# Four weight blocks a conditioning step, and a router with stationary weights in two column halves

## The chip, the cores and the metric

The kernel runs on one NeuronCore of a Trainium2 chip. The metric is the device time of one execution in microseconds; lower is better. Everything is float32. In the trace a float32 product on TensorE (PE) leaves two matmul records, a transpose one.

## The reference

Two layers of a hybrid backbone over 256 latent and 256 context tokens, 1024 wide. The two parts that the change touches are the conditioning and the router:

```python
s_lat = jax.nn.silu(c)
s_ctx = jax.nn.silu(c_ctx)
...
    mod = (s_lat @ ada_w[l] + ada_b[l])[:, None, :]
    mod_c = s_ctx @ ada_w[l] + ada_b[l]
    shift_a, scale_a, gate_a, shift_f, scale_f, gate_f = jnp.split(mod, 6, axis=-1)
...
    scores = jax.nn.sigmoid((t @ router).astype(jnp.float32))
    _, idx = lax.top_k(scores + bias.astype(jnp.float32), TOP_K)
```

`ada_w[l]` is 1024 x 6144, 24 MB a layer, and multiplies two vectors only: the conditioning of the latents and that of the context. `router` is 1024 x 64, for 512 tokens in layer 0 and 256 in layer 1. Each layer normalises, modulates and projects, runs three token mixers (retention, attention, gated MLP) that gated merges bring together, projects out, and ends with 64 small experts of which each token takes 6.

## The kernel before, in words

Activations lie feature by token: `xT` and `hT` hold 8 blocks of 128 features by 512 tokens. `layer_steps` writes out one order of steps for each layer; the five engines run it, each its own part. A step's products go into a bank of PSUM (a job); `jobs` numbers them, job n uses bank n % 8, and PE waits in `open_bank` until job n-8 has been emptied by ACT or DVE. `bank_full` counts finished jobs.

Weights come through `ring`, nine slots of 1 MB (`NS`), in order of first use, block p into slot p % 9. The SP queue loads block p only when the last step that used block p-9 has filled its bank (`await_free`), in order. Experts use the same ring after that.

Conditioning is done in steps `adaw` and `adat` (`step_adaw`, L748, and `step_adat`, L757, on PE). Before the change a layer has twelve of each. `adaw` takes two blocks of 256 columns. `silu_c` (two columns of conditioning, padded to 32) is stationary, the block is moving; the eight k-tiles go round the four column groups of 32, so that each group holds a partial sum of two k-tiles. ACT copies the bank to `ada_row` (128 x 512). `adat` multiplies each 128 columns of `ada_row` (stationary) by `sel`, which adds the four partial sums and turns the row into 128 partitions x 2. DVE adds `ada_b` into `mod` (L1534). The first norm of layer 0 needs the first 16 blocks of 128 of `mod`. In layer 0 four steps stand at the start among the turns of x (L670) and the mean squares (L700), eight in attention (`spread` and `weave` mix them with the branch-2 merges), and the twelve of layer 1 stand in the retention and branch-1 merges of layer 0.

```python
    if l + 1 < DEPTH:
        bulk = weave(ada_steps(l + 1, list(range(12))), bulk)
    out += spread([("ret", n) for n in range(len(ret_units(l)) + 2)], bulk)
```

The router (`step_rt`, L950) takes 128 tokens of `hT` as stationary and 64 columns of `router` as moving, 8 k-tiles a token tile. ACT makes `score` of the bank with tanh. Behind it PE turns `hT` for the expert rows (`h2`, L670) and does the shared expert (`sg`, `su`, `sd`), while DVE picks the experts.

Of the kernel before, what the change touches and what calls it, by code (L numbers as in the profile page):

```python
# [27 lines left out]
P = 128  # L28
# [34 lines left out]
CONST_COLS = {"ident": P, "iota1": P, "diff": 384, "tri": P, "tok": 8, "cos": 2 * ROPE, "sin": 2 * ROPE, "sel": 2}  # L63
# [17 lines left out]
def shape_constants():  # L81

    out = np.zeros((P, N_CONST), np.float32)

    def put(name, a):
        out[:, CONST_AT[name]:CONST_AT[name] + CONST_COLS[name]] = a

    p = np.arange(P)
    put("ident", np.eye(P))
    put("iota1", np.broadcast_to(np.arange(P) + 1, (P, P)))  # L90
    put("diff", np.arange(384)[None, :] - P - p[:, None])
    put("tri", (p[:, None] < p[None, :]))
    put("sel", (p[:, None] % 32 == np.arange(2)[None, :]))
# [52 lines left out]
def layer_steps(l):  # L146
# [22 lines left out]
    if l == 0:  # L169
        bulk = weave(ada_steps(0, list(range(4, 12))), bulk)  # L170
# [9 lines left out]
    out += [("out", m) for m in range(8)] + [("ms2",), ("norm", 2), ("rt",)] + [("h2", t) for t in mt]  # L180
# [9 lines left out]
def step_jobs(l, kind, *a):  # L190
# [42 lines left out]
    return [((kind, l) + a, "act" if kind in ("q", "k", "g", "ws", "u", "gv", "rt", "sg", "ms1", "ms2") else "dve")]  # L233


def step_pieces(l, kind, *a):

    if kind == "adaw":
        return [(a[0], "ada", 2 * a[1] + i) for i in range(2)]
# [16 lines left out]
    return {"ws": [(l, "ws")], "rt": [(l, "router")], "sg": [(l, "sg")], "su": [(l, "su")], "sd": [(l, "sd")]}.get(kind, [])  # L256


def backbone(nc, dram, out):
# [29 lines left out]
    with ExitStack() as ctx:  # L289
# [14 lines left out]
        ada_row = sb("ada_row", [P, 512])  # L304
# [103 lines left out]
        y_parts = [region(0, TOPK * D), region(15872, TOPK * D)]  # L408
        fin = region(0, 2, D)
# [256 lines left out]
        def _(pe):  # L666
# [52 lines left out]
            for l in range(DEPTH):  # L719
# [19 lines left out]
                def step_adaw(la, q):  # L739
# [3 lines left out]
                    for i in range(2):  # L743
                        p = piece_at[(la, "ada", 2 * q + i)]
                        await_loaded(pe, p)
                        for k in range(KT):
                            g = 32 * (k % 4)
                            last = mm(b[g:g + 32, 256 * i:256 * i + 256], silu_c[:, k, :], piece_view(p, KT, 256)[:, k, :],  # L748
                                      start=(k < 4), stop=(k >= 4))
                    last.then_inc(bank_full, 1)  # L750

                def step_adat(la, q):
# [3 lines left out]
                    for m in range(4):  # L756
                        last = mm(b[:, 2 * m:2 * m + 2], ada_row[:, P * m:P * m + P], const_cols("sel"), start=True, stop=True)  # L757
# [233 lines left out]
                def step_list(e):  # L991
# [3 lines left out]
                    for i in range(len(mt)):  # L995
# [7 lines left out]
                         "rt": step_rt, "h2": step_h2, "sg": shared("sg"), "su": shared("su"), "sd": step_sd, "pos": step_pos,  # L1003
# [149 lines left out]
        def _(act):  # L1153
# [54 lines left out]
            for l in range(DEPTH):  # L1208
# [15 lines left out]
                def step_adaw(la, q):  # L1224
                    if q or la:
                        await_full(act, ("adat", la, q - 1) if q else ("adat", la - 1, 11))
                    copy_out(("adaw", la, q), ada_row[:, :])
# [132 lines left out]

                def step_rt():
# [13 lines left out]
                def step_sg(m):  # L1375
# [5 lines left out]
                            "k": step_k, "g": step_g, "ret": step_ret, "out": step_out, "ms2": step_ms2, "norm": step_norm, "rt": step_rt, "h2": step_h2,  # L1381
# [53 lines left out]
        def _(dve):  # L1435
# [76 lines left out]
            for l in range(DEPTH):  # L1512
# [15 lines left out]
                def step_adat(la, q):  # L1528

                    if la == 0 and q == 0:  # L1530
                        await_emptied(dve, ("vec", 1))
                    b = await_full(dve, ("adat", la, q))
                    at = VEC_AT["ada_b"] + 4 * q
                    link(v.tensor_tensor(mod[:, la, 4 * q:4 * q + 4, :], b[:, 0:8].rearrange("p (m s) -> p m s", s=2),  # L1534
                                         vec[:, la, at:at + 4].unsqueeze(2).to_broadcast([P, 4, 2]), ALU.add))
                    dve.nop().then_inc(emptied["dve"], 1)
                    for g, name, first in ((gain1, "n1", 8), (gain2, "n2", 32)):
                        if 4 * q + 4 == first + KT:
# [3 lines left out]
                    if 4 * q + 4 == 24:  # L1542
# [501 lines left out]
```

## Time and profile before

| | us |
|---|---|
| median of 3 runs | 2792.06 (2790.34 to 2795.26) |
| span of the profiled execution | 2791.2 |
| PE busy (matmul) | 2423.6 (87%) |
| DVE busy | 764.5 (27%) |
| ACT busy | 482.0 (17%) |
| mean granted TensorE clock | 0.914 |

For the profiled execution only its span is listed, and no time of its own beside it. By stage, in us from the span's start: start and first norm 0 to 75, latents and first projections to 237, attention with branch-2 merges to 399, retention projections to 509, retention with branch-1 merges to 652, branch-0 merges and out projection to 811, router and shared expert to 877, experts to 1700, layer 1 up to its router to 2081, its experts from 2116 to the end.

A row of the timeline gives start, duration, engine, line, operation, output and inputs, the count that it merges, and in brackets the idle time of the engine before it with what ended it. Granted clock 1.00 is 2.4 GHz, 0.50 is 1.2 GHz.

### The profile page before, as it was taken

How to read it: one execution, taken by the hardware profiler on the slowest of the kernel's cores; microseconds unless marked ns; L12 is line 12 of the kernel's file. 1: busy time of each engine (PE TensorE's matmuls, PEld its weight loads, DVE VectorE, ACT ScalarE, POOL GpSimd, SP SyncE). 2: the span in 40 equal slices, each digit the busy share in tenths (PEclk: the TensorE clock that was granted, in tenths of full speed). 3: DMA queues.
4: the chain of work that ended last, by engine and by line, in shares of the span. 5: the costliest groups of instructions: out<-in, count | busy, mean ns of one | idle time of the engine just before them, and what ended most of it. 6: DMA issues, size and time to landing. Idle time of an engine off the chain costs nothing.

```text
span 2791.2 us, 39130 instructions
## 1 busy us (share of the span) xinstructions
PE 2423.6 (87%) x13062; PEld 1605.6 (58%) x13063; DVE 764.5 (27%) x2357; ACT 482.0 (17%) x1015; POOL 272.8 (10%) x320
## 2 busy tenths in 40 slices
PE   4997999999988988888888869899988778787876
PEld 3665556554455555556665567677876445444545
DVE  2324320231133323222223223431323222222221
ACT  3331111120020111111111113320221111111110
POOL 1000000000001111111111120000001111111111
PEclk9998999999989888999998889999999888888888
DMA  8132452464224888788878850432446888888884
GB/s 277 46 109 64 130 166 68 147 202 154 83 89 148 329 317 342 286 319 305 311 267 312 303 218 31 136 114 68 131 152 252 328 333 333 338 331 333 333 332 177
DMA packets 219213, 608.19 MB, mean 218 GB/s; under 512 B 22027, under 2 KB 152277, under 8 KB 169973
## 3 DMA queue, kind: packets, MB, share of 16 engines
q1 hardware_dynamic: 191584, 541.62, 53.5%
q0 software_dynamic: 26128, 61.07, 6.1%
q10 hardware_dynamic: 1412, 4.28, 0.4%
q8 instruction: 60, 0.98, 0.1%
q14 instruction: 29, 0.23, 0.0%
HBM read 596.94 MB, written 35.00 MB: 226 GB/s over the span
## 4 chain that ended last, share of the span: by engine, by line
PE 69%; DMA 15%; issue 6%; DVE 4%; POOLq 3%; ACT 2%; DVEq 1%; POOL 0%; ACTq 0%; SPq 0%
PE bank L677 25%; DMA area<-h_rows,idx 14%; PE bank L1044 11%; PE bank L685 6%; PE bank L670 6%; PE bank L1076 5%; PE bank L1051 2%; POOLq L548 2%; PE bank L1052 2%; PE bank L714 2%; PE bank L748 2%; DVE area L1876 1%; PE bank L824 1%; PE bank L802 1%; PE bank L839 1%
## 5 line engine op out<-in xcount | busy, mean ns | idle before, releaser
L1044 PE MATMUL bank<-ring,area 128*64 128x256 f32 x1840 | 530.1, 453 | 23.4 <-issue 19.9
L1045 PE MATMUL bank<-ring,area 128*64 128x256 f32 x1840 | 530.2, 453 | 0.0
L677 PE MATMUL bank<-hT,ring 128*128 128x512 f32 (+1 forms) x1408 | 481.1, 498 | 0.0
L670 PE MATMUL bank<-const,area 128*128 128x128 f32 (+3 forms) x1668 | 256.9, 301 | 227.8 <-DMA area<-h_rows,idx 183.9
L1044 PEld LDWEIGHTS bank<-ring,area 128*64 128x64 f32 x1840 | 291.8, 165 | 210.8 <-issue 125.3
L677 PEld LDWEIGHTS bank<-hT,ring 128*128 128x128 f32 x1408 | 265.6, 191 | 192.0 <-issue 176.3
L670 PEld LDWEIGHTS bank<-const,area 128*128 128x128 f32 (+3 forms) x1668 | 218.2, 189 | 266.2 <-issue 222.7
L1045 PEld LDWEIGHTS bank<-ring,area 128*64 128x64 f32 x1840 | 291.7, 165 | 0.0
L1076 PE MATMUL bank<-ring,area 128*64 128x512 f32 (+1 forms) x1024 | 267.2, 596 | 3.3 <-issue 2.5
L1956 POOL DMA_INDIRECT area<-h_rows,idx x130 | 123.6, 951 | 1425.6 <-DVEq L1826 1306.4
L677 PE MATMUL bank<-area,ring 128*128 128x512 f32 (+1 forms) x704 | 237.8, 486 | 2.8 <-issue 2.8
L1863 DVE SCALAR_TENSOR_TENSOR area<-area,wrow,bank 64x256 f32<-64x256 f32 (+1 forms) x128 | 61.7, 482 | 635.6 <-ACT area L1397 504.2
L1962 POOL DMA_INDIRECT expert_rows<-area,idx x128 | 118.1, 923 | 1034.5 <-issue 1034.5
L677 PEld LDWEIGHTS bank<-area,ring 128*128 128x128 f32 x704 | 133.4, 190 | 96.3 <-issue 87.3
L685 PE MATMUL bank<-ring,hT 128*128 128x256 f32 (+1 forms) x800 | 166.9, 370 | 6.2 <-ACT hT L1204 6.2
L685 PEld LDWEIGHTS bank<-ring,hT 128*128 128x128 f32 x800 | 147.4, 192 | 28.5 <-ACT hT L1204 6.3
L1397 ACT ACTIVATE area<-bank 128x256 f32<-128x256 f32 (+1 forms) x128 | 48.8, 381 | 645.5 <-PE bank L1045 505.4
L1173 ACT ACTIVATE area<-bank 128x512 f32<-128x512 f32 (+1 forms) x122 | 60.9, 505 | 517.5 <-PE bank L677 417.7
L1076 PEld LDWEIGHTS bank<-ring,area 128*64 128x64 f32 (+1 forms) x1024 | 84.6, 143 | 111.6 <-issue 96.9
L1854 DVE COPY area<-bank 128x512 f32<-128x512 f32 (+1 forms) x128 | 71.5, 558 | 229.7 <-PE bank L670 220.6
L1019 PEld LDWEIGHTS bank<-area 128*128 128x128 f32 (+1 forms) x756 | 86.5, 173 | 81.4 <-issue 81.2
L1393 ACT ACTIVATE area<-bank 128x512 f32<-128x512 f32 (+1 forms) x128 | 62.8, 491 | 375.9 <-PE bank L670 365.1
(192 smaller groups left out, 2039.4 us busy)
## 6 DMA issues: line engine op xcount, KB each, us to landing
ring<-in_moe_w_gate SPq DMA_DIRECT2D x128, 1024.0 KB, 7.0
ring<-in_moe_w_up SPq DMA_DIRECT2D x128, 1024.0 KB
ring<-in_moe_w_down SPq DMA_DIRECT2D x128, 1024.0 KB
ring<-in_w_in SPq DMA_DIRECT2D x52, 1024.0 KB, 7.9
ring<-in_ada_w SPq DMA_DIRECT2D x48, 1024.0 KB, 11.5
area<-expert_rows POOLq DMA_DIRECT2D x36, 512.0 KB, 7.6
ring<-in_w_out SPq DMA_DIRECT2D x8, 1024.0 KB, 9.0
ring<-in_w_br_gmlp SPq DMA_DIRECT2D x8, 512.0 KB, 8.4
```

Source lines behind the costliest of these rows:

```text
L670: return nc.tensor.transpose(dst, src, ident[0:n, 0:n])
L677: last = mm(b[:, 0:n], lhs[:, k, :], rhs[:, k, c:c + n], start=(k == 0), stop=(k == K - 1))
L685: last = mm(b[:, 0:n], lhs[:, k, P * tt:P * tt + P], rhs[:, k, :], start=(k == 0), stop=(k == K - 1))
L1019: last = mm(bank[7][0:cap, 256:259], pick[:, j, P * i:P * i + cap], entry(i, e), start=(i == 0), stop=(i == nm - 1))
L1044: mm(bank[4 + j][0:P // 2, 0:FF], x, wg[:, k, :], start=(k == 0), stop=(k == KT - 1))
L1045: last = mm(bank[4 + j][P // 2:P, 0:FF], x, wu[:, k, :], start=(k == 0), stop=(k == KT - 1))
L1076: last = mm(bank[2 + hf][o * hf:o * hf + m, :], hidT[:, j, cap * k:cap * k + m], wd[:, k, 512 * hf:512 * hf + 512], start=(k == 0), stop=( ...
L1393: af(x_rowsT[:, j, 0:4 * cap], bank[0][:, 0:4 * cap], ACT.Copy).then_inc(turned_act, 1)
L1854: v.tensor_copy(x_rowsT[:, j, 4 * cap:8 * cap], bank[1][:, 0:4 * cap]).then_inc(turned_dve, 1)
L1863: v.scalar_tensor_tensor(out=hid[0:m, j, :], in0=act_g[0:m, j, :], scalar=wrow[0:m, j:j + 1], in1=up, op0=ALU.mult, op1=ALU.mult).then_inc ...
L1956: pool.indirect_dma_start(out=x_rows[0:m, j, :], out_offset=None, in_=h2_dram[0:tokens(l), :], in_offset=bass.IndirectOffsetOnAxis(ap=idx[ ...
L1962: pool.indirect_dma_start(out=y_dram[0:TOPK * tokens(l), :], out_offset=bass.IndirectOffsetOnAxis(ap=idx[0:m, j, 2:3], axis=0), in_=y_rows ...
```

## The change

There are six conditioning steps a layer instead of twelve (`ADA_STEPS`). A step takes four blocks, one for each column group: all eight k-tiles of block i accumulate in partitions 32i to 32i+31, 256 columns wide. PE waits for all four blocks before the first product. `ada_row` is 128 x 256, and two products with a `sel` of eight columns turn 1024 values; DVE adds the bias in two operations. At the start x0 and x1 are turned ahead of the first step, both mean squares stand together, and the second step behind them. Elsewhere `spread` and `weave` mix six steps where they mixed twelve.

The router becomes two steps. In `lt` the router's 64 columns are stationary and the tokens move; even k-tiles go to column half 0, odd ones to half 1. ACT copies the bank to `logits`. In `rt` each 128 tokens of `logits` are stationary against `fold`, which adds the two halves and turns them back to token by expert.

```diff
-        ada = ada_steps(0, list(range(4)))
-        out += [("vec",)] + ada[:2] + [("x", 0), ("x", 1)] + ada[2:4] + [("x", 2), ("x", 3), ("ms1", 0)] + ada[4:6]
-        out += [("ms1", 1)] + ada[6:] + [("norm", 0), ("norm", 1)]
+        ada = ada_steps(0, list(range(2)))
+        out += [("vec",), ("x", 0), ("x", 1)] + ada[:2] + [("x", 2), ("x", 3), ("ms1", 0), ("ms1", 1)] + ada[2:]
+        out += [("norm", 0), ("norm", 1)]
...
-        bulk = weave(ada_steps(0, list(range(4, 12))), bulk)
+        bulk = weave(ada_steps(0, list(range(2, ADA_STEPS))), bulk)
...
-        bulk = weave(ada_steps(l + 1, list(range(12))), bulk)
+        bulk = weave(ada_steps(l + 1, list(range(ADA_STEPS))), bulk)
...
-        return [(a[0], "ada", 2 * a[1] + i) for i in range(2)]
+        return [(a[0], "ada", 4 * a[1] + i) for i in range(4)]
...
-                    for i in range(2):
-                        p = piece_at[(la, "ada", 2 * q + i)]
+                    quarters = [piece_at[(la, "ada", 4 * q + i)] for i in range(4)]
+                    for p in quarters:
                         await_loaded(pe, p)
-                        for k in range(KT):
-                            g = 32 * (k % 4)
-                            last = mm(b[g:g + 32, 256 * i:256 * i + 256], silu_c[:, k, :], piece_view(p, KT, 256)[:, k, :],
-                                      start=(k < 4), stop=(k >= 4))
+                    for k in range(KT):
+                        for i, p in enumerate(quarters):
+                            last = mm(b[32 * i:32 * i + 32, 0:256], silu_c[:, k, :], piece_view(p, KT, 256)[:, k, :],
+                                      start=(k == 0), stop=(k == KT - 1))
...
-                    for m in range(4):
-                        last = mm(b[:, 2 * m:2 * m + 2], ada_row[:, P * m:P * m + P], const_cols("sel"), start=True, stop=True)
+                    for m in range(2):
+                        last = mm(b[:, 8 * m:8 * m + 8], ada_row[:, P * m:P * m + P], const_cols("sel"), start=True, stop=True)
...
-                def step_rt():
+                def step_lt():
+
                     pe.wait_ge(h_ready, norm_at(("ms2", l)) + 1)
                     p = piece_at[(l, "router")]
                     await_loaded(pe, p)
+                    b = open_bank(pe, ("lt", l))
+                    for k in range(KT):
+                        g = N_EXP * (k % 2)
+                        last = mm(b[g:g + N_EXP, 0:nt], piece_view(p, KT, N_EXP)[:, k, :], hT[:, k, t0:T], start=(k < 2), stop=(k >= KT - 2))
+                    last.then_inc(bank_full, 1)
+
+                def step_rt():
+
+                    await_emptied(pe, ("lt", l))
                     b = open_bank(pe, ("rt", l))
-                    for i, t in enumerate(mt):
-                        for k in range(KT):
-                            last = mm(b[:, N_EXP * i:N_EXP * i + N_EXP], hT[:, k, P * t:P * t + P], piece_view(p, KT, N_EXP)[:, k, :],
-                                      start=(k == 0), stop=(k == KT - 1))
+                    for i in range(len(mt)):
+                        last = mm(b[:, N_EXP * i:N_EXP * i + N_EXP], logits[:, P * i:P * i + P], const_cols("fold"), start=True, stop=True)
                     last.then_inc(bank_full, 1)
...
+                def step_lt():
+                    copy_out(("lt", l), logits[:, 0:nt], lambda b: b[:, 0:nt])
```

How the rows of PE move, in three places. A row names line, operation, output and inputs, size, and how many follow each other.

PE at the start, before: the block products of `adaw` (L748) and turning products of `adat` (L757) among the turns of x (L670) and mean squares (L700).

```order
L748 MATMUL bank<-ring,silu_c 32x256 x16
L757 MATMUL bank<-const,ada_row 128x2 x4
L670 MATMUL bank<-const,area 128x128 x16
L748 MATMUL bank<-ring,silu_c 32x256 x16
L757 MATMUL bank<-const,ada_row 128x2 x4
L670 MATMUL bank<-const,area 128x128 x16
L700 MATMUL bank<-area,ones 128x256 x8
L748 MATMUL bank<-ring,silu_c 32x256 x16
L757 MATMUL bank<-const,ada_row 128x2 x4
L700 MATMUL bank<-area,ones 128x256 x8
L748 MATMUL bank<-ring,silu_c 32x256 x16
L757 MATMUL bank<-const,ada_row 128x2 x4
```

The same place now (L751, L760, L673 and L703 are the same four lines).

```order
L673 MATMUL bank<-const,area 128x128 x16
L751 MATMUL bank<-ring,silu_c 32x256 x32
L760 MATMUL bank<-const,ada_row 128x8 x2
L673 MATMUL bank<-const,area 128x128 x16
L703 MATMUL bank<-area,ones 128x256 x16
L751 MATMUL bank<-ring,silu_c 32x256 x32
L760 MATMUL bank<-const,ada_row 128x8 x2
```

The first turns of x have moved ahead of the first step, and no step stands between the two mean squares.

PE in the branch-1 merges of layer 0, before: a merge is L677 x8 (gate) and x4 (branch); L909, L921 and L670 are a retention step.

```order
L757 MATMUL bank<-const,ada_row 128x2 x4
L748 MATMUL bank<-ring,silu_c 32x256 x16
L757 MATMUL bank<-const,ada_row 128x2 x4
L677 MATMUL bank<-hT,ring 128x512 x8
L677 MATMUL bank<-area,ring 128x512 x4
L909 MATMUL bank<-area 128x256 x4
L921 MATMUL bank<-area 128x128 x4
L670 MATMUL bank<-const,area 128x128 x2
L748 MATMUL bank<-ring,silu_c 32x256 x16
L757 MATMUL bank<-const,ada_row 128x2 x4
```

And now, from merge 1 to the third step and merge 2.

```order
L680 MATMUL bank<-hT,ring 128x512 x8
L680 MATMUL bank<-area,ring 128x512 x4
L760 MATMUL bank<-const,ada_row 128x8 x2
L912 MATMUL bank<-area 128x256 x4
L924 MATMUL bank<-area 128x128 x4
L673 MATMUL bank<-const,area 128x128 x2
L751 MATMUL bank<-ring,silu_c 32x256 x32
L680 MATMUL bank<-hT,ring 128x512 x8
```

A step directly followed by its own turning products occurs twice in this stage now, four times before.

PE at the router of layer 0, before: L950 is the router, L670 the turns of h2, the last row the shared expert.

```order
L677 MATMUL bank<-area,ring 128x512 x8
L700 MATMUL bank<-area,ones 128x512 x2
L950 MATMUL bank<-ring,hT 128x64 x32
L670 MATMUL bank<-const,hT 128x128 x32
L677 MATMUL bank<-hT,ring 128x512 x16
```

The same place now, with L954 for `lt` and L962 for the folding.

```order
L680 MATMUL bank<-area,ring 128x512 x8
L703 MATMUL bank<-area,ones 128x512 x2
L954 MATMUL bank<-hT,ring 64x512 x8
L962 MATMUL bank<-const,area 128x64 x4
L673 MATMUL bank<-const,hT 128x128 x32
L680 MATMUL bank<-hT,ring 128x512 x16
```

Thirty-two products became eight and four, with a copy by ACT between them. On ACT the table load for tanh stood directly behind the last operation on `hT`; it now stands behind this copy.

## Rows read from the trace of the kernel before

**Rows 1.** The page, chain that ended last: share of the span by engine.

```profile
PE 69%; DMA 15%; issue 6%; DVE 4%; POOLq 3%; ACT 2%; DVEq 1%; POOL 0%; ACTq 0%; SPq 0%
```

**Rows 2.** Timeline of PE in the branch-1 merges of layer 0.

```profile
587.06 1.02 PE L757 MATMUL bank<-const,ada_row 128*128 128x2 f32 x8 [0.87 <-ACT ada_row L1173]
588.01 1.93 PE L748 MATMUL bank<-ring,silu_c 128*32 128x256 f32 x32
589.88 1.13 PE L909 MATMUL bank<-area 128*128 128x256 f32 x4
...
603.15 0.95 PE L757 MATMUL bank<-const,ada_row 128*128 128x2 f32 x8
604.03 1.93 PE L748 MATMUL bank<-ring,silu_c 128*32 128x256 f32 x32
```

**Rows 3.** Timeline of PE at the routers of layers 0 and 1.

```profile
811.36 13.91 PE L950 MATMUL bank<-ring,hT 128*128 128x64 f32 x64 [11.64 <-ACT hT L1204]
825.07 5.07 PE L670 MATMUL bank<-const,hT 128*128 128x128 f32 x32
...
2087.75 3.44 PE L670 MATMUL bank<-const,hT 128*128 128x128 f32 x16
```

**Rows 4.** Timeline of the start, PE, ACT and DVE.

```profile
27.13 1.93 PE L748 MATMUL bank<-ring,silu_c 128*32 128x256 f32 x16 [12.01 <-DMA ring<-in_ada_w]
...
39.24 1.95 PE L670 MATMUL bank<-const,area 128*128 128x128 f32 x16
...
41.28 0.71 ACT L1192 ACTIVATE area<-xT 128x256 f32<-128x256 f32 x2
...
49.22 0.71 ACT L1192 ACTIVATE area<-xT 128x256 f32<-128x256 f32 x2
...
55.20 1.93 PE L748 MATMUL bank<-ring,silu_c 128*32 128x256 f32 x32
...
59.06 0.17 DVE L1534 TENSOR_TENSOR mod<-bank,vec 128x8 f32<-128x8 f32 x1 [8.36 <-PE bank L757]
...
65.25 10.00 PE L685 MATMUL bank<-ring,hT 128*128 128x256 f32 x35 [6.23 <-ACT hT L1204]
```

**Rows 5.** The experts' products in column halves, and their weight loads.

```profile
2121.76 0.38 PE L1044 MATMUL bank<-ring,area 128*64 128x256 f32 x1
2121.76 0.38 PE L1045 MATMUL bank<-ring,area 128*64 128x256 f32 x1
...
1505.60 1.89 PE L1076 MATMUL bank<-ring,area 128*64 128x512 f32 x8
...
L1076 PEld LDWEIGHTS bank<-ring,area x1024: 132/137/338, 891.6 to 2746.9; 128*64 128x64 f32 x152, 128*128 128x128 f32 x19
```

**Rows 6.** Fourth block and x: issue, and time to landing (last number).

```profile
10.41 11.39 SPq L644 DMA_DIRECT2D ring<-in_ada_w  x1
...
DMA to landing us min/median/max: 22.7/22.7/22.7
...
8.79 0.72 POOL L1941 DMA_DIRECT2D area<-in_x  x1
...
area<-in_x POOLq DMA_DIRECT2D x1, 1024.0 KB, 11.2
```

**Rows 7.** Timeline of PE in attention, 256 keys, two steps back to back.

```profile
277.45 0.41 PE L670 MATMUL bank<-const,area 128*128 128x128 f32 x2 [0.40 <-ACT area L1304]
```

**Rows 8.** DMA issues, median us to landing: 380 to 520 us, then 500 to 660 us.

```profile
ring<-in_ada_w SPq DMA_DIRECT2D x10, 1024.0 KB, 5.5
...
ring<-in_ada_w SPq DMA_DIRECT2D x18, 1024.0 KB, 11.2
```

**Rows 9.** Windows: stretch, length, busy by engine, granted clock, DMA share, GB/s.

```profile
65.00:70.00 5.00, 4.75 (x11) 3.85 (x12) 4.55 (x9) 3.35 (x9) 0.00 (x0) 0.50 0.01 2
70.00:75.00 5.00, 5.00 (x25) 4.37 (x25) 0.54 (x2) 0.15 (x1) 0.00 (x0) 0.98 0.00 0
...
815.00:820.00 5.00, 5.00 (x26) 5.00 (x25) 0.00 (x0) 0.00 (x0) 0.00 (x0) 0.50 0.00 0
```

More of the change, by code:

```diff
@@ L62 @@
 ROW_BC = {"qn": QK, "kn": NOPE, "kr": ROPE, "lng": GW, "lnb": GW, "bs": GW, "bias": N_EXP, "dec": 8}
-CONST_COLS = {"ident": P, "iota1": P, "diff": 384, "tri": P, "tok": 8, "cos": 2 * ROPE, "sin": 2 * ROPE, "sel": 2}
+CONST_COLS = {"ident": P, "iota1": P, "diff": 384, "tri": P, "tok": 8, "cos": 2 * ROPE, "sin": 2 * ROPE, "sel": 8, "fold": N_EXP}
+ADA_STEPS = 6
 def offsets(sizes):
@@ L92, in shape_constants @@
     put("tri", (p[:, None] < p[None, :]))
-    put("sel", (p[:, None] % 32 == np.arange(2)[None, :]))
+    put("sel", (p[:, None] == 32 * (np.arange(8)[None, :] // 2) + np.arange(8)[None, :] % 2))
+    put("fold", (p[:, None] % N_EXP == np.arange(N_EXP)[None, :]))
     tok = np.arange(TT)[None, :] * P + p[:, None] - BIG
@@ L176, in layer_steps @@
     if l + 1 < DEPTH:
-        bulk = weave(ada_steps(l + 1, list(range(12))), bulk)
+        bulk = weave(ada_steps(l + 1, list(range(ADA_STEPS))), bulk)
     out += spread([("ret", n) for n in range(len(ret_units(l)) + 2)], bulk)
     out += [("merge", m, 0) for m in range(8)]
-    out += [("out", m) for m in range(8)] + [("ms2",), ("norm", 2), ("rt",)] + [("h2", t) for t in mt]
+    out += [("out", m) for m in range(8)] + [("ms2",), ("norm", 2), ("lt",), ("rt",)] + [("h2", t) for t in mt]
     out += [("sg", m) for m in range(2)] + [("pos",), ("cnt",)] + [("su", m) for m in range(2)]
@@ L232, in step_jobs @@
         return []
-    return [((kind, l) + a, "act" if kind in ("q", "k", "g", "ws", "u", "gv", "rt", "sg", "ms1", "ms2") else "dve")]
+    return [((kind, l) + a, "act" if kind in ("q", "k", "g", "ws", "u", "gv", "lt", "rt", "sg", "ms1", "ms2") else "dve")]
 def step_pieces(l, kind, *a):
     if kind == "adaw":
-        return [(a[0], "ada", 2 * a[1] + i) for i in range(2)]
+        return [(a[0], "ada", 4 * a[1] + i) for i in range(4)]
     if kind == "c":
@@ L255, in step_pieces @@
         return [(l, "wo", a[0] // 2)]
-    return {"ws": [(l, "ws")], "rt": [(l, "router")], "sg": [(l, "sg")], "su": [(l, "su")], "sd": [(l, "sd")]}.get(kind, [])
+    return {"ws": [(l, "ws")], "lt": [(l, "router")], "sg": [(l, "sg")], "su": [(l, "su")], "sd": [(l, "sd")]}.get(kind, [])
 def backbone(nc, dram, out):
@@ L303, in backbone @@
         silu_c = sb("silu_c", [P, KT, 32])
-        ada_row = sb("ada_row", [P, 512])
+        ada_row = sb("ada_row", [P, 256])
         mod = sb("mod", [P, DEPTH, 48, 2])
@@ L1225, in step_adaw @@
                     if q or la:
-                        await_full(act, ("adat", la, q - 1) if q else ("adat", la - 1, 11))
-                    copy_out(("adaw", la, q), ada_row[:, :])
+                        await_full(act, ("adat", la, q - 1) if q else ("adat", la - 1, ADA_STEPS - 1))
+                    copy_out(("adaw", la, q), ada_row[:, :], lambda b: b[:, 0:256])
                 def step_ms1(s):
@@ L1532, in step_adat @@
                     b = await_full(dve, ("adat", la, q))
-                    at = VEC_AT["ada_b"] + 4 * q
-                    link(v.tensor_tensor(mod[:, la, 4 * q:4 * q + 4, :], b[:, 0:8].rearrange("p (m s) -> p m s", s=2),
-                                         vec[:, la, at:at + 4].unsqueeze(2).to_broadcast([P, 4, 2]), ALU.add))
+                    at = VEC_AT["ada_b"] + 8 * q
+                    for m in range(2):
+                        last = v.tensor_tensor(mod[:, la, 8 * q + m:8 * q + 8:2, :], b[:, 8 * m:8 * m + 8].rearrange("p (i s) -> p i s", s=2),
+                                               vec[:, la, at + m:at + 8:2].unsqueeze(2).to_broadcast([P, 4, 2]), ALU.add)
+                    link(last)
                     dve.nop().then_inc(emptied["dve"], 1)
                     for g, name, first in ((gain1, "n1", 8), (gain2, "n2", 32)):
-                        if 4 * q + 4 == first + KT:
+                        if 8 * q + 8 == first + KT:
                             n_g = vec[:, la, VEC_AT[name]:VEC_AT[name] + KT].unsqueeze(2).to_broadcast([P, KT, 2])
```

7 lines of the change are left out of this document (4 added, 3 removed).

## The prediction

> **What bounds the kernel now.** I read the chain of waits first: 69% of the span lies on the matmul queue and 15% on DMA [rows 1]. Most of that is attention, projections and experts, which the change leaves alone. So the question is local: where do the conditioning steps and the router stand on the matmul queue, and does PE wait there or work? A change of 0.2% (5.6 us) is about what a measurement of this kernel can tell from none.
>
> Then the rows of the conditioning code. The turning products, `ada_row` against `sel`, are 96 in the run, four in each of 24 steps. Four of them hold PE from 603.15 to 604.03, so 0.22 us each [rows 2], although only 2 columns move. They cost that because each loads a full 128-column stationary. The reader should see the same in the router: 64 records of 64 moving columns fill 13.9 us [rows 3].
>
> Third, the start, which is a chain. PE idles until the second weight block has landed at 27.13, takes that half step at half speed (8 products in 1.93 us, where 16 take 1.93 at 55.20), turns x, squares, and ends with `mod` at 59.06; the first projection begins at 65.25 [rows 4]. Fourth, the branch-1 merges of layer 0 (509 to 652 us): PE has work throughout, and its only waits near conditioning are of 0.87 us, where a turning product follows its own step at once [rows 2].
>
> **The change, part by part.** The blocks multiplied stay 384 products per run, four column groups in rotation before and after. A step of 16 takes 1.87 us in the stream (588.01 to 589.88 [rows 2]). Four products at once need 0.43, two passes of 256 columns at 0.21 each, as the experts' 512 columns in halves (8 records in 1.89 [rows 5]) give them, so 1.71 of it is streaming and 0.15 is paid once per step. A new step is then 3.42 + 0.15 = 3.57 us. Ten of the steps that go lie outside the start, so 1.5 us of the gain below are this overhead.
>
> *Start: +2.0 us.* Steps 0 and 1 now need four blocks each. The fourth block was issued at 10.41 and landed 22.7 later, at 33.1 [rows 6]; before, PE could begin at 27.13. x was issued at 8.8 and landed 11.2 later, at 20.0 [rows 6], so its first 16 turns move into the idle time ahead and are off the path. From 33.1: 32 products at half speed 7.2 (four times the 1.93 less its tails); copy and hand-over 0.65; two turning products 0.6; this gives 41.6. Turning x2 and x3 to the first square took 2.04 (39.24 to 41.28), so squares begin at 43.7, against 41.28. The two norms now follow each other with no step between. The second took 6.0 us, from 49.22 to the step at 55.20; the first 7.9, with the copy of a step in it [rows 4]; between the two I take 6.4. So the last step begins at 56.1, takes 3.57, then copy and two products 1.3: `mod` at 61.0 against 59.06. If the clock rises inside the first step it is +0.8; if DMA lands later, +4.
>
> *Attention of layer 0: -4.2.* Eight steps become four: 24 turning products fewer, 24 x 0.22 = -5.2; four step overheads, -0.6. Against that, bulk now follows each second attention step. With 256 keys a step is too short to cover ACT's softmax, and where two stand back to back PE waited 0.40 [rows 7]. Such pairs go from one to five: +1.6. With 512 keys I charge nothing: ACT and DVE finish under the longer step.
>
> *Branch-1 merges: -6.0.* Twelve steps become six: 36 products fewer, -7.8; six overheads, -0.9. A turning product stands directly behind its step twice, not four times, and the copy is half as wide, for which I take 0.65 where PE idled 0.87: 4 x 0.87 less 2 x 0.65 = -2.2. The new cost is the ring. It has nine slots and block p loads when block p-9 is done. The fourth block of the third step takes the slot of the gate weights of merges 0 and 1, free only after merge 1. Between that and the step lie two turning products and one retention step: 0.44, four products of 256 columns at 0.43, four of 128 at 0.22, two turns at 0.11, 3.3 us and 3.4 with hand-overs. A block issued to an idle queue lands in 5.5 us [rows 8]. So PE waits 2.0. The fourth block of the last step waits for merge 5 in the same way, with two turning products, eight of 128 columns and two turns between, 2.5 us: it waits 2.9. Together +4.9. Every other step has a whole merge, 12 products of 512 columns or 10.3 us, between the freeing of its last block and its start. The upper bound is the median of this stage, 11.2 us [rows 8], taken with queued loads: 7.8 + 8.7 = 16.5. The lower is 0. I take 5.5, since the queue has been served by then. Behind a waiting step stand only merges, whose weights land 3 us behind the late block and before it ends.
>
> *Router of layer 0: -7.1.* 32 products took 811.36 to 825.07, 13.7 us, at a granted clock of 0.50 (the 1.2 GHz level) to the end [rows 3, 9]. Now 8 products of 512 columns go in two column halves. Four such products take 1.8 us in the experts at full clock [rows 5], so 3.4, at half 6.8. After its idle time before 65.25 the clock stood at 0.50 up to 70 us, under dense work, and at 0.98 from 70 to 75 [rows 9]; with the same here the eight take 5.9. Then ACT copies (0.9 with the hand-over, PE idle), and four folding products take 0.9. The turns of h2 start at 819.0 instead of 825.07. They then run at full clock, 3.9 instead of 4.9. The table load for tanh, formerly hidden, falls behind the copy: 1.3 beside 0.9 of folding, so tanh ends at 819.6, not late for anything on PE. If the clock stays at half all through, only -2.
>
> In the Trainium skill, TensorE: Matmul & The Clock Gate, Part 3, weight loads overlap running matmuls only if their row groups differ; all these share the 128 rows. By that rule the 16 loads of 137 ns [rows 5] would add 2.2 us in each layer. The trace disagrees: four products of this form take 1.89 with their eight loads, of which 1.71 is streaming.
>
> *Router of layer 1: -2.5.* Half as many products, 16, took half as long, 6.9, up to 2087.75. Now 3.6 + 0.65 + 0.9 = 5.1, so -1.8; and the 16 turns behind (3.44 [rows 3]) may meet the higher clock earlier, at most -1.5 more. I take half of that. ACT's and DVE's own savings cost PE nothing and give nothing: both are mostly idle.
>
> Sum: 2.0 - 4.2 - 6.0 - 7.1 - 2.5 = **-17.8 us**. Later stages should shift as a whole, because expert weights cannot run ahead by more than nine blocks. The profiled span is 2791.2, 0.9 below the median of the runs, 2792.06, so I subtract from the median: **2774.3 us**.
>
> **Rivals.** *The ring starves PE* for the 16.5 us above: -17.8 - 4.9 + 16.5 = -6.2, and if each wait drops the clock for 5 us, another +5: 2785.9 to 2790.9. For: four blocks now come free at once. Against: no row of before has PE waiting for a block after the start.
>
> *The router keeps half the clock*: gain 2 in layer 0 and 1.8 in layer 1, so -12.0: 2780. For: it stayed at 0.50 through the old router. Against: dense columns raised it at 70.
>
> *Weight loads of the router are not hidden*: if each of its 16 loads of 137 ns stood between two products in both layers, +4.4, so 2778.7. Against: four products with eight loads take 1.89 [rows 5], which leaves no room for 1.1 of loads. This is the skill's rule above.
>
> *The column groups no longer run together*, the case on the slower side. Each group now streams from another slot of the ring. If only two overlapped, 32 products would take 16 x 0.43 = 6.8 us, +3.3 on each of 12 steps, +39: 2813. It decides for slower once a step takes over 3.57 + 17.8/12 = 5.1. Against: the experts' gate and up products read two slots and start together at 2121.76 [rows 5].
>
> **How the numbers follow.** Forecast 0.72, half clock in the router 0.12, starved ring 0.10, unhidden loads 0.02, groups apart 0.04. The likeliest gives 2774.3. Its own bounds are the start (-1.2 to +2), ring (-4.9 to +4), clock in the routers (-2 to +6), some 2768 to 2783; with part of the starved case, and a little for what I have not seen, 2766 to 2786. Faster: the forecast, the clock and loads cases and a little of the starved one, 0.88; same 0.08; slower 0.04.
>
> **What would show it.** A step of 32 products near 3.6 us and a pair of turning products near 0.44. `mod` complete near 61. Waits for ring blocks of 2 to 3 us ahead of the third and last step of the branch-1 merges, and nowhere else after the start. The router's eight products at some 6 us with h2's turns starting 7.6 us after them. The forecast is wrong if a step takes over 5 us, if PE waits for blocks in attention, or if the time between router and experts does not shrink.

## The result, and the profile after

The changed kernel takes 2770.47 us (median of 6 runs, 2758.21 to 2781.14) where the kernel before took 2793.66 beside it (6 runs, 2785.84 to 2799.33). The ratio is 0.9923, 95% interval 0.99 to 0.9946. The profiled execution took 2771.84, with a span of 2769.5 at a mean granted clock of 0.921. The forecast was 2774.3.

The page first: busy time by engine, and the chain that ended last by engine. It answers to [rows 1].

```profile
PE 2380.8 (86%) x12866; PEld 1568.4 (57%) x12867; DVE 763.1 (28%) x2357; ACT 472.3 (17%) x1005; POOL 271.9 (10%) x320
...
PE 68%; DMA 16%; issue 6%; DVE 4%; POOLq 3%; ACT 2%; DVEq 1%; POOL 0%; ACTq 0%; SPq 0%
```

PE is busy 43 us less than before (2423.6), and the span is 22 us shorter. The two differ, so the page alone doesn't say where the time went; stage marks on PE's timeline do. In us, from the same instruction to the same instruction of both profiles:

| stretch | before | after | difference | forecast |
|---|---|---|---|---|
| to the first projection | 65.25 | 65.48 | +0.2 | +2.0 |
| first projection to first attention score | 140.37 | 139.76 | -0.6 | 0 |
| first attention score to first retention product | 303.33 | 304.28 | +0.95 | -4.2 |
| first retention product to router of layer 0 | 302.41 | 298.01 | -4.4 | -6.0 |
| router of layer 0 | 18.61 | 11.68 | -6.9 | -7.1 |
| shared expert and lists of layer 0 | 47.34 | 47.34 | 0 | 0 |
| experts of layer 0 to router of layer 1 | 1203.6 | 1196.4 | -7.2 | 0 |
| router of layer 1 | 10.17 | 6.22 | -3.95 | -2.5 |
| from there to the end | 700.17 | 700.37 | +0.2 | 0 |

The row of 1200 us is code that the change leaves alone. PE is busy for 1066.6 us of it before and for 1049.4 after, at a mean granted clock of 0.92 and 0.93. In nine more profiles below, one of them with the old router and one with the old conditioning, it takes 1191.9 to 1201.0. So the 1196.4 of the change is ordinary, and the 1203.6 of before is the longest of eleven. Of the kernel before there is one profile only; whether its 7 us are chance is not shown. The runs of one kernel differ by more: the six of the change lie 23 us apart.

PE's timeline at the start, answering to [rows 4]:

```profile
20.14 3.68 PE L673 MATMUL bank<-const,area 128*128 128x128 f32 x16 [11.56 <-DMA area<-in_x]
33.36 6.20 PE L751 MATMUL bank<-ring,silu_c 128*32 128x256 f32 x64 [9.54 <-DMA ring<-in_ada_w]
40.05 0.61 PE L760 MATMUL bank<-const,ada_row 128*128 128x8 f32 x4 [0.50 <-ACT ada_row L1184]
...
54.27 3.66 PE L751 MATMUL bank<-ring,silu_c 128*32 128x256 f32 x64
58.59 0.58 PE L760 MATMUL bank<-const,ada_row 128*128 128x8 f32 x4 [0.66 <-ACT ada_row L1184]
```

The fourth block arrived at 33.36 (forecast 33.1) and x's turns lie ahead of it in what was idle time. A step of 32 products takes 3.66, within 0.1 of the 3.57 worked out. The copy of the half-wide row leaves PE idle 0.66, for which 0.65 had stood.

PE's timeline in the branch-1 merges, answering to [rows 2]: six steps, two of which wait for the ring.

```profile
550.89 3.66 PE L751 MATMUL bank<-ring,silu_c 128*32 128x256 f32 x64 [2.25 <-DMA ring<-in_ada_w]
...
581.43 3.66 PE L751 MATMUL bank<-ring,silu_c 128*32 128x256 f32 x64
585.75 0.58 PE L760 MATMUL bank<-const,ada_row 128*128 128x8 f32 x4 [0.66 <-ACT ada_row L1184]
...
621.93 5.35 PE L751 MATMUL bank<-ring,silu_c 128*32 128x256 f32 x64 [2.96 <-DMA ring<-in_ada_w]
627.21 7.13 PE L680 MATMUL bank<-hT,ring 128*128 128x512 f32 x16
...
637.83 0.51 PE L760 MATMUL bank<-const,ada_row 128*128 128x8 f32 x4
638.20 1.96 PE L680 MATMUL bank<-hT,ring 128*128 128x512 f32 x4
```

The third and the last step wait 2.25 and 2.96 for their blocks, as forecast (2.0 and 2.9). But the same 64 records take 5.35 behind the second wait. The window there, with the columns of [rows 9], shows why: the granted clock is 0.54 with PE fully busy.

```profile
622.00:625.00 3.00, 3.00 (x32) 1.86 (x36) 0.28 (x1) 0.00 (x0) 0.00 (x0) 0.54 1.10 350
```

PE's timeline at the two routers, answering to [rows 3]:

```profile
807.53 6.54 PE L954 MATMUL bank<-hT,ring 128*64 128x512 f32 x16 [11.63 <-ACT hT L1215]
814.77 1.10 PE L962 MATMUL bank<-const,area 128*128 128x64 f32 x8 [0.70 <-ACT area L1184]
815.71 3.66 PE L673 MATMUL bank<-const,hT 128*128 128x128 f32 x32
...
2062.91 3.49 PE L954 MATMUL bank<-hT,ring 128*64 128x256 f32 x16 [6.67 <-ACT hT L1215]
2066.88 0.66 PE L962 MATMUL bank<-const,area 128*128 128x64 f32 x4 [0.49 <-ACT area L1184]
2067.37 1.92 PE L673 MATMUL bank<-const,hT 128*128 128x128 f32 x16
```

13.9 us of products with 64 moving columns have become 6.54, 0.70 of idle time and 1.10. The turns of `hT` behind them take 3.66 where they took 5.07, because the clock had risen inside the eight products: it stood at 0.50 up to 812.5 and at 1.00 from 813.5.

### The profile page after: what moved, and what is told of

The parts are those of the page before. It is cut to its first block, busy times and chain, and to the rows that moved or that the text cites. A ratio compares the mean times of both kernels' runs of the same rounds, so it can differ in the third digit from the quotient of the medians.

```text
span 2769.5 us, 38705 instructions
## 1 busy us (share of the span) xinstructions
PE 2380.8 (86%) x12866; PEld 1568.4 (57%) x12867; DVE 763.1 (28%) x2357; ACT 472.3 (17%) x1005; POOL 271.9 (10%) x320
## 4 chain that ended last, share of the span: by engine, by line
PE 68%; DMA 16%; issue 6%; DVE 4%; POOLq 3%; ACT 2%; DVEq 1%; POOL 0%; ACTq 0%; SPq 0%
PE bank L680 25%; DMA area<-h_rows,idx 14%; PE bank L1055 11%; PE bank L688 6%; PE bank L673 6%; PE bank L1087 5%; POOLq L551 2%; PE bank L1062 2%; PE bank L751 2%; PE bank L717 2%; PE bank L1063 2%; DVE area L1892 1%; DMA ring<-in_ada_w 1%; PE bank L827 1%; PE bank L805 1%
## 5 line engine op out<-in xcount | busy, mean ns | idle before, releaser
L1055 PE MATMUL bank<-ring,area 128*64 128x256 f32 x1840 | 514.0, 442 | 22.2 <-issue 22.1
L1056 PE MATMUL bank<-ring,area 128*64 128x256 f32 x1840 | 514.2, 442 | 0.0
L673 PE MATMUL bank<-const,area 128*128 128x128 f32 (+3 forms) x1668 | 261.2, 304 | 254.8 <-DMA area<-h_rows,idx 197.4
L1055 PEld LDWEIGHTS bank<-ring,area 128*64 128x64 f32 x1840 | 285.0, 161 | 200.8 <-issue 111.5
L673 PEld LDWEIGHTS bank<-const,area 128*128 128x128 f32 (+3 forms) x1668 | 220.1, 189 | 295.6 <-issue 236.3
L1056 PEld LDWEIGHTS bank<-ring,area 128*64 128x64 f32 x1840 | 284.9, 161 | 0.0
```

The source lines that it names most:

```text
L673: return nc.tensor.transpose(dst, src, ident[0:n, 0:n])
L1055: mm(bank[4 + j][0:P // 2, 0:FF], x, wg[:, k, :], start=(k == 0), stop=(k == KT - 1))
L1056: last = mm(bank[4 + j][P // 2:P, 0:FF], x, wu[:, k, :], start=(k == 0), stop=(k == KT - 1))
```

## Experiments

**Repeating the change.** To know how far profiles of one kernel differ, the changed kernel ran again.

> The changed kernel, once more. Theory 1: the steps outside the experts take the same time in every execution but for the granted clock, and the 7.3 us by which layer 0's experts were shorter than before came from the clock by chance; so the start of the first projection, the start of retention, the end of the branch-1 merges and the router repeat within 3 us (65.5, 509.5, 648.7, 11.7 long), while the 823 us of experts differ by several us either way. Theory 2: the shorter experts' stage is an effect of the change; then it repeats, 7 us shorter than before's. Time by both 2758 to 2781.

Measured: 2770.32 (2768.17 to 2779.83, 6 runs), ratio 0.9932 [0.9908, 0.9956]. Attention stretch 304.19 and ring waits 2.07 and 2.83 repeat. The routers differ by the clock alone: layer 0 takes 10.12 instead of 11.68, because the clock rose 3 us earlier, and layer 1 takes 8.49 instead of 6.22, because it stayed at 0.50 until the turns were done. The expert stretch takes 1199.65, 3.3 longer than in the first profile.

**One part alone.** First the conditioning without the router:

```diff
-... ("norm", 2), ("lt",), ("rt",)] + [("h2", t) for t in mt]
+... ("norm", 2), ("rt",)] + [("h2", t) for t in mt]
...
-                    for i in range(len(mt)):
-                        last = mm(b[:, N_EXP * i:N_EXP * i + N_EXP], logits[:, P * i:P * i + P], const_cols("fold"), start=True, stop=True)
+                    for i, t in enumerate(mt):
+                        for k in range(KT):
+                            last = mm(b[:, N_EXP * i:N_EXP * i + N_EXP], hT[:, k, P * t:P * t + P], piece_view(p, KT, N_EXP)[:, k, :],
```

> Conditioning as changed, router as before. Theory 1: the router and h2's turns take 18.6 us in layer 0 and 10.2 in layer 1 again, 10.9 more than with the change, so about 12 us of the 23 remain: 2781, ratio 0.995 to 0.997. Rival (the conditioning is worth nothing, since attention began retention no earlier than before and the ring gave back the rest): 2789 to 2794, ratio 1.00.

Measured: 2784.02 (2775.19 to 2788.35, 12 runs), ratio 0.997 [0.9955, 0.9984], so about 8 us. Then the router without the conditioning (`adaw`, `adat`, `ada_steps` and `sel` as before, `lt` and `fold` added):

> Router as changed, conditioning as before. Theory 1: 11.7 us from the router to the end of h2's turns in layer 0 where 18.6 stood, 6.2 in layer 1 where 10.2 stood, nothing else moves: -10.9, so 2783, ratio 0.996. Rival (the router carries all of the gain): -22, ratio 0.992.

Measured: 2778.94 (2763.35 to 2787.26, 12 runs), ratio 0.9955 [0.9935, 0.9975], so about 12 us. Taken from the ratios the parts are 8.4 and 12.6 us, 21.0 in sum, and both together 21.5 and 19.0 in the two sets of runs: within the intervals they add. Forecast were 8.2 and 9.6. The intervals (4.5 to 12.6 us, and 7.0 to 18.1) are too wide to judge a term by; the stages do that. The retention stretch shrinks by 4.75 (302.41 to 297.66) with the new conditioning alone and by nothing with the new router alone (302.41), the router of layer 0 goes to 11.14 with the new router alone and stays at 18.13 without it.

**Freeing the gate slot earlier.** Are the waits of 2.25 and 2.96 due to the ring slot of the gate weights? A merge has two jobs, the gate product first. The edit lets that slot go after the first.

```diff
-                last_use[piece] = len(jobs) - 1
+                last_use[piece] = len(jobs) - 1 - (piece[1] == "gate")
```

> The changed kernel, with the slot of a merge's gate weights given back when the gate product is full and not when the branch product is, 3.4 us earlier. Theory 1: the waits for ring blocks of 2.25 and 2.96 us ahead of the third and the last step of the branch-1 merges go to 0, and with them the fall of the clock that followed the second (5.35 us for a step that takes 3.66): 5 to 7 us less than the change from 509.5 to 648.7, 132 to 134 where it took 139.2; time 2763 to 2766. Rival (the waits come from the DMA rate, not from when the slot is free): the two waits stay above 1.5 us each and the time stays at 2770.

Measured: 2761.47 (2759.01 to 2775.76, 6 runs), ratio 0.991 [0.9883, 0.9937]. PE's timeline at the same two steps:

```profile
540.86 3.66 PE L751 MATMUL bank<-ring,silu_c 128*32 128x256 f32 x64
...
608.88 3.66 PE L751 MATMUL bank<-ring,silu_c 128*32 128x256 f32 x64
```

Both waits are gone and so is the 5.35. From the first retention product to the router it takes 290.98 instead of 298.01: 7.0 us, of which 5.2 are the waits and 1.7 the slow step. The same kernel once more:

> The kernel with the gate slot freed early, again, beside the one with the spread attention. Theory 1: no wait for ring blocks after the start, branch-1 merges in 121.3 us to the last turning product where the change takes 128.3; time 2760 to 2766. Rival (its 9 us under the change were the clock of one set of runs): 2770.

Measured: 2765.18 (2758.0 to 2776.08, 6 runs), ratio 0.9922 [0.9899, 0.9945]; the stretch 290.98 again, in a profile of 2756.1. So the stage gains 7 us, while the medians of the runs, 2761 and 2765 against 2770, are 5 to 9 lower and their intervals overlap with the change's: for the whole kernel this edit is shown by the profiles, not by the ratios.

**One group after the other.** Do the four column groups run together because neighbours in the instruction stream are in different groups?

```diff
-                    for k in range(KT):
-                        for i, p in enumerate(quarters):
+                    for i, p in enumerate(quarters):
+                        for k in range(KT):
```

> The changed kernel, with the 32 products of a conditioning step in another order: all eight k-tiles of block 0 in column group 0, then those of block 1 in group 1, and so on, so that neighbours share a group. Theory 1 (the four groups run together because neighbours lie in different groups): 32 x 0.43 = 13.7 us a step instead of 3.6, +10 us on each of 12 steps less the 5 us of ring waits, which the longer steps cover: 2880 to 2895. Rival (PE overlaps the groups whatever the order, or did not overlap them before): a step stays at 3.6 us and the time at 2770.

Measured: 2866.94 (one run). PE's timeline:

```profile
582.39 11.50 PE L751 MATMUL bank<-ring,silu_c 128*32 128x256 f32 x64
612.70 11.47 PE L751 MATMUL bank<-ring,silu_c 128*32 128x256 f32 x64 [2.16 <-DMA ring<-in_ada_w]
```

The clock is 1.00 in the first of these rows. The groups are not even fully apart: the recorded expectation for that was 13.7, and why it is 2.2 less stays open. 32 products in this order take 11.5 us where they take 3.66 in rotation: 7.8 more, and twelve steps of that are 94 of the 96.5 us by which the kernel is longer. The rival in which the groups fall apart thus has its price, and by which edit it would come. The ring waits stay (2.16 here, 2.96 at the last step, at 707.21), though every step is 8 us longer: they depend only on what lies between the merge that frees the slot and the step that needs the block.

**The router in one half.** Is the router's gain the new orientation (`router` stationary, 512 tokens moving) or the two column halves? The copy and the folding, not shown here, use 64 partitions accordingly.

```diff
-                        g = N_EXP * (k % 2)
-                        last = mm(b[g:g + N_EXP, 0:nt], ..., start=(k < 2), stop=(k >= KT - 2))
+                        last = mm(b[0:N_EXP, 0:nt], ..., start=(k == 0), stop=(k == KT - 1))
```

> The changed kernel, with the router's eight products all in column half 0 (64 partitions), then folded from 64 partitions. Theory 1 (the split halves the products' time): they take 9 to 10 us in layer 0 where 6.5 stood and 6 in layer 1 where 3.5 stood, +5 in all. Rival (the gain of the router comes from the exchange of the operands alone): 6.5 and 3.5 us again.

Measured: 2776.52 (one run). PE's timeline at both routers:

```profile
809.35 9.86 PE L953 MATMUL bank<-hT,ring 128*64 128x512 f32 x16 [11.63 <-ACT hT L1214]
...
2069.19 6.27 PE L953 MATMUL bank<-hT,ring 128*64 128x256 f32 x16 [6.67 <-ACT hT L1214]
```

9.86 and 6.27 stand against 6.54 and 3.49, so in these profiles the halves are worth 3.3 and 2.8 us. But the clock differs between the forms. Windows, first of the kernel before, then of this one:

```profile
811.36:825.07 13.71, 13.71 (x65) 13.71 (x65) 0.00 (x0) 1.25 (x1) 0.00 (x0) 0.50 0.00 0
```

```profile
809.35:815.00 5.65, 5.65 (x7) 1.67 (x8) 0.00 (x0) 0.00 (x0) 0.00 (x0) 0.50 0.00 0
815.50:819.20 3.70, 3.70 (x9) 0.96 (x7) 0.00 (x0) 0.00 (x0) 0.00 (x0) 1.00 0.00 0
```

Count each microsecond at full clock twice, which puts everything at half clock, and the old form takes 13.9 us in layer 0 and 7.1 in layer 1, this one 14.1 and 7.2, and the two halves 7.3 and 3.8. At one clock the orientation thus brings nothing and the halves bring it all, although the weight loads (the second busy time of a row) fill the whole window of the old form and only 1.67 of 5.65 us here. The 4.1 us between 13.91 and 9.86 are the clock's: with the tokens moving it rose 2.6 to 5.8 us behind the router's first product of layer 0, in ten profiles; with the old router, in two, 15.5 and 16.6 us behind it. That is an association. It doesn't hold in layer 1, where in five of the nine profiles with two halves the clock stayed at 0.50 about as long as with the old router.

**Spreading the attention.** The stretch that had not gained is attention. In the change `spread` puts 16 bulk steps behind 30 attention steps, so behind every second one; before it was 24. Now the first 12 of the 30, which have 256 keys, get one each, and the 18 behind them the other four. Nothing is added or left out; only the order differs. This edit alone, on the change:

```diff
-    out += att[:4] + [("sv", t) for t in mt] + spread(att[4:], bulk)
+    n = 12 if l == 0 else 0
+    out += att[:4] + [("sv", t) for t in mt] + spread(att[4:4 + n], bulk[:n]) + spread(att[4 + n:], bulk[n:])
```

It ran first together with the freed gate slot:

> The kernel with the gate slot freed early, and in layer 0's attention a merge, a block step or a turning pair behind each of the twelve next attention steps with 256 keys, the last four such pieces over the 18 steps with 512. Theory 1 (two short attention steps back to back let PE wait for the softmax, and those waits are 0.4 to 0.6 us each): the five waits on ACT go, 2 to 3 us less before retention begins, and the clock falls in attention are fewer; 2758 to 2761. Rival (the waits move elsewhere or the clock falls are not tied to them): attention takes as long as in the kernel before this one, 2761 to 2764.

Measured: 2747.8 (2744.94 to 2751.1, 5 runs), ratio 0.9844 [0.9825, 0.9864]: 10 us below what the better theory had for it (2758 to 2761). A repeat:

> Spread attention and the gate slot freed early, again. Theory 1: the stretch of attention repeats at 290 us and the branch-1 merges at 121.3; time 2745 to 2752, 5 to 7 below the kernel with the spread alone. Rival (its 2748 was the clock of one set): 2755 to 2762.

Measured: 2750.46 (2744.63 to 2754.15, 5 runs), ratio 0.9854 [0.9834, 0.9874]. And the new order without the freed slot:

> The changed kernel with the spread attention alone, the gate slot given back as in the change. Theory 1 (what attention earned was lost to its own order: waits and the clock falls around them): from the first attention score to the start of retention 290 to 292 us where the change took 304.3, with at most 20 us at half clock where it had 37.5; the two ring waits in the branch-1 merges stay at 2 and 3 us; time 2753 to 2758. Rival (the clock in attention is chance, as it is among the experts): 298 to 304 us for that stretch and 2763 to 2770.

Measured: 2758.51 (2749.81 to 2764.47, 6 runs), ratio 0.9883 [0.9862, 0.9905]. Attention takes 289.94, 14.3 us less than in the change.

First the waits. PE's timeline in attention, of the change: the rows with a wait for ACT, without the first wait of 11 us that every kernel has, and the step behind the first of them:

```profile
232.31 0.41 PE L673 MATMUL bank<-const,area 128*128 128x128 f32 x2 [2.91 <-ACT area L1315]
233.05 5.35 PE L751 MATMUL bank<-ring,silu_c 128*32 128x256 f32 x64
...
240.52 0.41 PE L673 MATMUL bank<-const,area 128*128 128x128 f32 x2 [0.40 <-ACT area L1315]
...
253.78 0.41 PE L673 MATMUL bank<-const,area 128*128 128x128 f32 x2 [0.56 <-ACT area L1315]
...
274.69 0.41 PE L673 MATMUL bank<-const,area 128*128 128x128 f32 x2 [0.56 <-ACT area L1315]
...
281.21 0.41 PE L673 MATMUL bank<-const,area 128*128 128x128 f32 x2 [0.40 <-ACT area L1315]
...
384.04 0.63 PE L673 MATMUL bank<-const,area 128*128 128x128 f32 x4 [0.70 <-ACT area L1315]
```

And of the new order alone, at the place of the first two:

```profile
226.02 0.38 PE L674 MATMUL bank<-const,area 128*128 128x128 f32 x2
226.24 0.56 PE L843 MATMUL bank<-area 128*128 128x64 f32 x4
226.73 3.66 PE L752 MATMUL bank<-ring,silu_c 128*32 128x256 f32 x64
...
244.09 0.41 PE L674 MATMUL bank<-const,area 128*128 128x128 f32 x2
```

PE no longer waits there, and the step takes 3.66 where it took 5.35. PE also has waits for DVE in this stretch, and these did not go. Three of them, in the new order alone:

```profile
262.34 0.63 PE L674 MATMUL bank<-const,area 128*128 128x128 f32 x4 [1.21 <-DVE area L1636]
...
318.86 0.63 PE L674 MATMUL bank<-const,area 128*128 128x128 f32 x4 [0.45 <-DVE area L1636]
...
321.05 0.63 PE L674 MATMUL bank<-const,area 128*128 128x128 f32 x4 [1.17 <-DVE area L1636]
```

Then the clock. Windows, first of the change, then of the new order with the freed slot (the whole stretch and three pieces of it):

```profile
205.24:509.52 304.28, 283.24 (x1184) 164.15 (x1185) 83.83 (x236) 47.27 (x108) 0.00 (x0) 0.94 0.33 105
232.00:238.00 6.00, 5.69 (x67) 3.33 (x70) 1.73 (x8) 0.73 (x4) 0.00 (x0) 0.72 0.01 3
256.00:264.00 8.00, 8.00 (x28) 5.51 (x27) 3.13 (x13) 1.73 (x5) 0.00 (x0) 0.57 0.01 2
298.00:306.00 8.00, 8.00 (x24) 5.12 (x23) 2.13 (x7) 1.38 (x3) 0.00 (x0) 0.58 0.00 0
```

```profile
204.80:494.98 290.18, 273.48 (x1185) 158.50 (x1185) 83.42 (x236) 47.30 (x108) 0.00 (x0) 0.97 0.35 110
232.00:238.00 6.00, 6.00 (x22) 3.27 (x21) 1.40 (x6) 0.95 (x3) 0.00 (x0) 1.00 0.84 265
256.00:264.00 8.00, 6.79 (x84) 4.32 (x83) 3.31 (x11) 1.52 (x5) 0.00 (x0) 1.00 0.81 254
298.00:306.00 8.00, 8.00 (x29) 4.30 (x27) 1.33 (x4) 0.82 (x2) 0.00 (x0) 1.00 0.97 320
```

In the change PE is fully busy from 256 to 264 and from 298 to 306 and yet gets 0.57 and 0.58 of its clock; each time small waits lie just ahead (0.56 and 1.09 before 256, 0.45 and 1.19 before 298). In the new order the clock is 1.00 there. The same account for the profiles: the stretch less PE's busy time in it, and the time spent at half clock between 204 and 400 us (two-microsecond windows, each counted as twice its missing share). Half of the latter is what it costs, apart from 8 to 9 us of it in which PE is idle in every kernel. The kernel with the products group by group has other step lengths and is left out.

| kernel | stretch | idle | half clock |
|---|---|---|---|
| before | 303.33 | 19.82 | 27.4 |
| router only | 301.61 | 19.82 | 23.9 |
| change | 304.28 | 21.04 | 37.5 |
| change again | 304.19 | 21.04 | 37.5 |
| conditioning only | 301.88 | 21.38 | 30.7 |
| gate slot | 297.79 | 21.17 | 23.9 |
| gate slot again | 302.88 | 20.98 | 34.1 |
| router in one half | 305.83 | 21.12 | 40.9 |
| new order, three profiles | 289.94 to 290.18 | 16.70 | 17.0 to 17.1 |

The sums close. Change against before: work -5.8 at the forecast's prices, idle +1.2, half clock (37.5 - 27.4)/2 = +5.05, together +0.45 for a measured +0.95. New order against before: -5.8 - 3.1 - 5.15 = -14.1 for -13.4.

The 17 us of the new order all lie around the first wait of 11 us; from 226 to 490 its clock is 1.00 in all three profiles, though waits of 1.21, 0.45 and 1.17 stand there as they do in the change (1.09, 0.45, 1.19). So such a wait alone doesn't bring the fall. The new order also keeps attention steps with 256 keys from standing back to back, and no run separates that from the waits that went with it.

## Why the prediction was right and wrong

**The total** came within 4 us, and its sign and order of size came by their own reasons. But one term failed, and luck covered it: without the 7 us of the expert stretch, which no term had, the stages of the two profiles sum to -14.5. The medians of the two sets of runs stand 23 and 21 us apart. The stages thus don't account for all of what the medians say; the scatter among the runs of one kernel is large enough for the rest, but nothing shows that it is that.

**Attention of layer 0, -4.2: this step failed.** "Such pairs go from one to five: +1.6" was right as idle time: four pairs of 256 keys wait 0.40 or 0.56, and the stretch's whole idle time rose by 1.2. The turning products went as priced: a pair holds PE for 0.37 us (637.83 to 638.20), for which 0.44 had stood. What had no term was the clock. I had priced a clock fall after a wait only for the ring (in a rival), and not for the order of steps in attention, where in this profile it cost 5 us and ate the gain. The six profiles with this packing in the table spent 23.9 to 40.9 us at half clock (mean 34.1), the two with the old one 27.4 and 23.9, and the three with the new order 17.0 to 17.1. By these means the packing costs (34.1 - 25.7)/2 = 4.2 us of clock, and the mean stretch is 302.8 against 302.5, so the whole gain is gone. Two profiles of the old packing are few, and one of the six lies as low as they do, so the size of that cost is uncertain. What the three profiles of the new order show is that the order of the same steps decides it. "With 512 keys I charge nothing" missed two new waits, of 0.70 and 0.45, small again.

**Branch-1 merges, -6.0: mechanism right, size off by the clock.** The two ring waits came where they were forecast and as long (2.25 and 2.96 for 2.0 and 2.9), and the freed gate slot removed both. The stretch gained 4.4; the missing 1.6 are the step of 5.35 at 621.93. "if each wait drops the clock for 5 us" stood in the rival alone, and belonged in the main sum at a smaller price: in the five profiles that have both waits and this order of products, six of the ten steps behind them took 5.09 to 5.35, the others 3.66, so 0.6 x 1.6 us a wait, 2 us for both.

**Router of layer 0, -7.1:** measured -6.9. The eight products took 6.54 for 5.9, since the clock rose later; over nine profiles with this code they took 4.98 to 6.54. Copy and folding came as priced (0.70 idle, 0.94 to the turns), and the turns went from 4.9 to 3.5. The 3.4 for the eight products at full clock was near: counted at full clock they took 3.6. That the clock would rise within them came true in all nine; why it did is an association only.

**Router of layer 1, -2.5:** -3.95 here, with the turns at full clock (1.92 for 3.44). In five of nine profiles with this router it took 8.49, in the other four 6.2 to 6.3, by the clock alone. The mean, 7.5, gives -2.7 against the before profile. Halving the unknown was right.

**The start, +2.0:** measured +0.2. The clock rose inside the first step (6.20 for 7.2), as the +0.8 bound had allowed, and from the first squares to the last step it took 11.7 where 12.4 had stood. `mod` was complete at 59.45, not 61.

**The rivals.** The ring starving PE did not come: 5.2 of waits for 16.5. The router did leave half clock. The column groups stayed together, and the test order shows what would have undone it. The weight loads of the router are hidden, which the third rival had in doubt. In layer 1 of the repeated change the clock was 0.50 throughout, and the 16 records took 3.68. At half clock eight products of 256 columns in two halves, four pairs of 0.86, stream for 3.4, by the price of [rows 5]. Their 16 loads, which took 225 ns each at half clock in the change's own profile, would add 3.6 if they stood between the products, and 0.3 is left. By the Trainium skill (TensorE: Matmul & The Clock Gate, Part 3, the mechanism) loads overlap running products only where the row groups differ; here all use the same 128 rows. The trace does not agree. The sentence ahead of that rule also lets a load into the background weight buffer run ahead, and nothing in the trace speaks against that.

## What to carry to other kernels

Price a new order of steps on the matmul queue by what the clock does in it, not only by the waits that it adds: here the new packing of attention added 1.2 us of idle time and went with 4 to 5 us of lost clock. Before crediting an operand exchange, compare both forms at one clock: at one clock the router's products gained by the two column halves alone. When a change takes bulk work out of a stage whose other steps need cover, count how many of those steps now stand back to back, and move what is left of the bulk to the shortest ones; here this order alone was worth 12 us in the medians, more than the conditioning change that called for it. A ring slot is freed by the last job of its step, so a block that is used early in the step can be let go earlier.

## What was not expected of the hardware

Four column groups overlap fully only if the stream alternates between them. 32 products of 32 x 256 take 3.66 us in rotation and 11.5 us group by group, 0.11 and 0.36 a product; on paper both orders do the same, and the four blocks' products sit in different columns in both. The Trainium skill (TensorE: Matmul & The Clock Gate, Part 3, the mechanism) has matmuls start and end in program order without reordering. The second order fits that, as one group's eight products follow each other and share its columns, and the trace adds what it costs.

The granted clock fell to half in a stretch where the waits were much shorter than those that I had looked for: PE was fully busy in 256 to 264 us, behind waits of 0.56 and 1.09, and got 0.57. That is an association. The kernel with the freed gate slot spent 23.9 us at half clock in one profile and 34.1 in the other, with the same waits, and the new order has waits of 1.21 and 1.17 with no fall. What brings the fall remains open, and no run isolates it. Also open is why the untouched expert stretch varies by 12 us between profiles.

The version with the spread order and the freed gate slot beats both kernels: 2748 and 2750 us in two sets of runs, ratios 0.9844 [0.9825, 0.9864] and 0.9854 [0.9834, 0.9874] to the kernel before. Against the order alone (2758.51) that is 8 and 11 us less, for a stretch that is 6.8 shorter (121.27 for 128.09, up to the last turning products); the rest is within the scatter.
